# Hybrid decoder step: order of the query normalisation's first tiles, and where the first attention pair begins among dense pieces

## What is computed

```python
def trunk_layer(x, ...):
    xn = rmsnorm(x, norm_mix)
    lru_x, lru_g, q, k, v = jnp.split(xn @ w_in, SPLITS, axis=-1)
    xc = causal_conv(x_ext, w_conv, b_conv)
    hs, h_T = rg_lru(xc, pos, h0, ...)
    y_lru = (hs * jax.nn.gelu(lru_g)) @ w_branch_lru

    q = rmsnorm(q.reshape(B, T, N_ATT_HEADS, HEAD_DIM), q_gain)
    k = rmsnorm(k.reshape(B, T, N_ATT_HEADS, HEAD_DIM), k_gain)
    ...
        outs.append(dilated_attn_prompt(qg, kg, vg, tab, window, dil))
    ...
    o = combine_groups(outs)
    y_att = o @ w_branch_att
    g_lru, g_att = jnp.split(jax.nn.sigmoid(xn @ w_merge + b_merge), 2, axis=-1)
    x = x + (g_lru * y_lru + g_att * y_att) @ w_o
    gate, up = jnp.split(rmsnorm(x, norm_ffn) @ w_ffn_in, 2, axis=-1)
    return x + (jax.nn.silu(gate) * up) @ w_ffn_out, ...
```

## Time and profile before

| | |
|---|---|
| median of three runs | 2072.51 us (2072.47 to 2077.44) |
| the profiled execution | 2071.17 us |
| its span | 2069.4 us |
| PE busy | 2014.0 us (97%) |
| DVE, ACT, GpSimd busy | 905.9, 509.3, 552.1 us |
| PE clock granted, mean over the span | 0.993 of full |

### The profile page before, as it was taken

The page is one execution under the profiler, slowest core; times in us unless marked ns, Lnnn a source line. Parts: engine busy times, 40 slices in busy tenths (PEclk is TensorE's granted clock), DMA queues, the critical chain, the costliest instruction groups (busy, mean ns, idle before and its releaser), DMA issues.

```text
span 2069.4 us, 32282 instructions
## 1 busy us (share of the span) xinstructions
PE 2014.0 (97%) x12884; PEld 1952.3 (94%) x12884; DVE 905.9 (44%) x919; ACT 509.3 (25%) x726; POOL 552.1 (27%) x325
## 2 busy tenths in 40 slices
PE   7999998999989999999989899999999999999999
PEld 7999997999979999999978899999999999999999
DVE  6666677777762332222266553433311233212331
ACT  5366653333333433333311111201000000000000
POOL 2323332222211111111122143323323232323322
PEclk9999999999999999999999999999999999999999
DMA  5211111222223323334286361111111111111112
GB/s 200 97 44 43 43 46 61 93 90 81 101 97 135 116 97 136 114 111 149 87 307 236 125 239 51 44 48 51 41 51 41 51 42 49 51 41 51 41 59 84
DMA packets 71595, 188.45 MB, mean 91 GB/s; under 512 B 9313, under 2 KB 28796, under 8 KB 70780
## 3 DMA queue, kind: packets, MB, share of 16 engines
q1 hardware_dynamic: 41456, 136.97, 19.5%
q10 hardware_dynamic: 30092, 50.81, 6.7%
HBM read 145.09 MB, written 45.81 MB: 92 GB/s over the span
## 4 chain that ended last, share of the span: by engine, by line
PE 89%; DVE 6%; ACT 1%; issue 1%; DMA 1%; POOL 0%; ACTq 0%; SPq 0%; DVEq 0%; POOLq 0%
PE ups L472 64%; PE ups L600 13%; PE ups L625 3%; PE ups L650 3%; PE aux L637 2%; DVE x L1335 1%; PE aux L538 1%; PE aux L559 1%; PE ups L486 1%; PE aux L614 0%; DVE x L1489 0%; DVE x L1259 0%; DMA x<-o_s 0%; DVE x L1280 0%; ACT x L1076 0%
## 5 line engine op out<-in xcount | busy, mean ns | idle before, releaser
L472 PE MATMUL ups<-big,wsp 128*128 128x344 f32 x9216 | 1477.3, 321 | 9.1 <-POOL wsp L450 6.6
L472 PEld LDWEIGHTS ups<-big,wsp 128*128 128x128 f32 x9216 | 1459.4, 189 | 24.0 <-issue 16.9
L448 POOL CAST wsp<-wraw 128x1024 fp32r<-128x1024 f32 (+2 forms) x160 | 167.8, 1049 | 1485.0 <-issue 724.0
L450 POOL TENSOR_TENSOR wsp<-wraw,wsp 128x1024 fp32r<-128x1024 f32 (+2 forms) x160 | 384.0, 2400 | 12.8
L600 PE MATMUL ups<-big,wsp 128*128 128x344 f32 x1728 | 291.8, 324 | 0.0
L600 PEld LDWEIGHTS ups<-big,wsp 128*128 128x128 f32 x1728 | 272.7, 189 | 5.3 <-issue 5.2
L1335 DVE RECIPROCAL x<-x 128x1024 f32<-128x1024 f32 x24 | 157.3, 6553 | 74.4 <-ACT x L1006 74.4
L1372 DVE SCALAR_TENSOR_TENSOR x<-ups,ext 128x256 f32<-128x256 f32 (+1 forms) x96 | 48.0, 542 | 235.4 <-PE aux L637 147.4
L1181 ACT ACTIVATE ext<-ext 128x1032 f32<-128x1032 f32 x22 | 23.6, 1071 | 482.5 <-DVE ext L1589 482.4
L1591 DVE TENSOR_TENSOR ext<-ups,ext 128x1032 f32<-128x1032 f32 x22 | 27.1, 1233 | 215.4 <-PE ups L472 215.4
L1605 DVE TENSOR_TENSOR x<-ups,x 128x1032 f32 x24 | 29.6, 1233 | 203.6 <-PE ups L472 203.6
(11 more groups left out here) (190 smaller groups left out, 1147.9 us busy)
## 6 DMA issues: line engine op xcount, KB each, us to landing
wraw<-w_in SPq DMA_DIRECT2D x52, 512.0 KB, 3.4
wraw<-w_ffn_in SPq DMA_DIRECT2D x44, 512.0 KB, 3.2
out_qkv<-x ACTq DMA_DIRECT2D x28, 512.0 KB, 2.7
ext<-out_qkv SPq DMA_DIRECT2D x24, 512.0 KB, 4.3
x<-x_T SPq DMA_DIRECT2D x16, 516.0 KB, 8.2
x<-gate_s SPq DMA_DIRECT2D x16, 516.0 KB, 4.1
wraw<-w_merge SPq DMA_DIRECT2D x16, 512.0 KB, 4.9
wraw<-w_ffn_out SPq DMA_DIRECT2D x16, 512.0 KB, 3.5
```

The source lines that it names most:

```text
L448: nc.gpsimd.tensor_copy(hi, raw).then_inc(w_hi, 1)
L450: nc.gpsimd.tensor_tensor(lo, raw, hi.bitcast(F32), ALU.subtract).then_inc(w_split[slot], 1)
L472: ins = nc.tensor.matmul(ups[:, slot, c, 0:CH], wsp[:, slot, w, k, :], src[:, a, k, c * CH:(c + 1) * CH], start=(k == 0 and w + a == 0), s ...
```

## The change

Four edits, all of order:

- PE: in unit (1, 1), the sums of (0, 1) come before its first chunk and not after it; in the first attention pair 16 pieces (not 8) come ahead of the last sums, and `FIRST_PIECES` has 24 pieces (not 16) ahead of the value transposes, then 8, 4, 4, 3, 3 and 2 (before: 8, 8, 6, 4, 4 and 2).
- ACT: unit (0, 1) is copied out, squared and rounded ahead of the first root, with a wait for `z_done` that the old order did not need; the two output DMAs go behind that root.
- DVE: the first iteration of the loop is written out with both square differences one place earlier: those of (0, 1) ahead of the reciprocal of (0, 0), those of (1, 0) ahead of the reciprocal of (0, 1).

```diff
-        FIRST_PIECES = (16, 24, 32, 38, 42, 46, 48)
+        FIRST_PIECES = (24, 32, 36, 40, 43, 46, 48)
...
             unit("qk", 1, 0, big1, parts=(1, 2))
-            unit("qk", 1, 1, big1, parts=(0,))
             stats(1, 0)
-            unit("qk", 1, 1, big1, parts=(1,))
+            unit("qk", 1, 1, big1, parts=(0, 1))
             stats(0, 1)
...
-                    pieces(0, 8)
+                    pieces(0, 16 if first else 8)
                     if first:
                         stats(1, 11)
-                        pieces(8, marks[0])
+                        pieces(16, marks[0])
...
             evac(0, 0)
+            act.wait_ge(z_done, KT + 1)
+            evac(0, 1)
             act.wait_ge(lru_done, KT)
+            root(0, 0)
             act.dma_start(O["lru_out"], sout[:]).then_inc(out_done, 16)
             act.dma_start(O["state_out"], stc[:]).then_inc(out_done, 16)
-            root(0, 0)
-            evac(0, 1)
...
-            with dve.Fori(0, 11) as i:
-                step.loop(i, 2)
+            square_low(0, 1)
+            normed_qk(0, 0)
+            square_low(1, 0)
+            normed_qk(0, 1)
+            with dve.Fori(1, 11) as i:
+                step.loop(i, 2, 1)
                 normed_qk(i, 0)
                 square_low(i, 1)
                 normed_qk(i, 1)
                 square_low(i + 1, 0)
-            step.end(11)
+            step.end(10)
```

## The result

| | before | after |
|---|---|---|
| median of 13 runs | 2073.03 us (2070.33 to 2077.44) | 2077.46 us (2074.99 to 2083.23) |
| ratio | | 1.0023, 95% interval 1.0013 to 1.0032 |
| profiled execution, its span | 2071.17, 2069.4 us | 2075.36, 2073.6 us |

The change makes the kernel slower, by 4.4 us between the medians and by 4.8 by the ratio (2.7 to 6.6 by its interval). I had forecast 2072.3, practically no change, and a range up to 2076.8, which the time missed by 0.7 us. Two single executions in the experiments, 2198 us of the kernel before and 2464 us of part 2 filled, had a far lower granted clock (0.85 and 0.75) and are left out of the ratios.

A forecast was written before the change was run, and what follows sets the result against it. TensorE was taken to bound the kernel (89% of the chain), time counting only where it waits or runs at a lower clock. Terms -4.5 + 4.3 = -0.2 us from 2072.51 gave 2072.3 us, range 2067.8 to 2076.8.

The forecast's parts named there:

- Part 1: Start of the query-key stage: second sums without wait, 0.5 us before the third, 4.7 before the fourth; net gain 4.5 us.
- Part 2: First attention head pair: no wait for the last sums, 4.9 us for the scores, then a new wait; net loss 4.3 us.
- the gate of 4.32 on ACT's copy: First pair: pieces behind the first scores wait for ACT's copy L1046, made after the exponentials; forecast 4.2 us.
- The rival that the gate does not bind: First pair: copy L1046 isn't what pieces 24 to 32 wait for, so no cost there; 2068.0 us, chance 10%.
- the line for DVE: Query-key stage: DVE owes two reciprocals with L1337 (6.55 + 1.29 each) and one L1270, ending at 335.7; new wait 4.7 us.
- the one where I bounded the overlap with GpSimd by 0 and 0.5 and took 0: First pair: GpSimd's next weight split may lie beside DVE's last L1337; bounds 0 and 0.5 us, taken as 0.
- The gain of part 1 doesn't come: Rival, query-key stage: DVE makes the sums of (1,1) no earlier than before; +4.3, 2076.8 us, chance 12%.
- The clock stays low through the pair: Rival, first attention pair: after two long waits PE's clock stays low; +14, 2086 us, chance 5%.
- the 2.2 + 2.3 of the forecast: Prices of a clock fall at long PE waits: 2.2 us in the query-key stage, 2.3 us in the first attention pair.

The follow-up runs named there:

- part 2 filled: Only the attention change on the kernel before, with unread matmuls in PE's waits (16, 36, 34, 24): 1.0011, median 2075.02 us without the execution of 2464 us.
- the experiment without it: Changed kernel with no pieces behind the first scores, FIRST_PIECES = (24, 24, 33, 38, 44, 47, 48): 0.9992 of the kernel before, median 2071.93 us.
- the square difference in between: Changed kernel with DVE's square difference of (1,0) between reciprocal and product of (0,1), not ahead of the reciprocal: 1.0000 of the kernel before, median 2073.57 us.
- part 2 alone: The kernel before with only the attention change, 16 pieces ahead of the last sums and the new FIRST_PIECES: 1.0050, median 2083.7 us of 5 runs.
- the repaired kernel: Changed kernel with square difference between reciprocal and product, three GpSimd splits held back, no pieces behind first scores: 0.9965 of the kernel before, median 2066.11 us.
- one filled kernel: Changed kernel with matmuls that no one reads in PE's three long waits (36, 36, 24): 1.0002 of the kernel before, median 2072.93 us.

## Why the prediction was right or wrong

- **The order of the waits, right.** Part 1: no wait, 0.92 (forecast 0.5), then a new long one. Part 2: no wait for the last sums, the score wait, the gate of 4.32 on ACT's copy, then three waits at the transposes. The rival that the gate does not bind fell with the row itself, and the experiment without it gave 5.1 us of the pair back.
- **Part 1's size, wrong: 1.7 us of gain and not 4.5.** The step that failed is the line for DVE with L1337 at 1.29 us throughout. I noted GpSimd for part 2 alone and did not ask what it does when the unit (1,1) ends: its split is released by that unit's end, at 323.8, and DVE was by then so late that L1337 stood there, at 325.3. Before, L1337 of (0,1) was done, at 326.8, long before its split began at 335.2. L1337 lost 0.53 and 2.0 us. The first of these could be read ahead of the run: I had put L1337 of (0,0) at 312.7 to 314.1, and the trace before has this there:

```profile
311.05 2.40 POOL L450 TENSOR_TENSOR wsp<-wraw,wsp 128x1024 fp32r<-128x1024 f32 x1
```

  For the two together the fourth sums came 2.4 us later than forecast; with 0.5 for a longer fall of the clock (2.08 and 13.1 us behind the wait against 2.07 and 12.5), 4.5 becomes 1.6. With the splits held back the stage gained 4.4.
- **Part 2's size, wrong: 7.0 us of loss and not 4.3.** The step that failed is the one where I bounded the overlap with GpSimd by 0 and 0.5 and took 0. It was 1.21 us (L1337 2.50). The bound came from one row, 1.75 us beside 0.67 us of overlap, without asking how much overlap there could be. My own figures had some: L1337 due at 595.65 + 0.97 = 596.6, the split's end near 597. In that time (the attention's first piece laid on that of before, 1.97 us later) the split ended at 597.9 and L1337 began at 596.5. Second, the 24 matmuls behind the gate took 6.75 us for 5.54: +1.2. That there are two waits ahead of them and not one does not explain it, since three other kernels with the same two waits had 5.51, 5.53 and 5.70; here is that with the splits held back:

```profile
605.44 5.53 PE L612 MATMUL ups<-big,wsp 128*128 128x344 f32 x24 [4.33 <-ACT x L1059]
```

  In those three the clock fell a second time later in the pair, and the pair was no shorter for it (61.10 us with the square difference in between). So 5.54 was a fair price for these matmuls, and what was left out is a second fall behind the wait of 1.75 us or a longer first one. Another 0.4 lies between DVE's last instruction before the scores and the scores (0.45 us, 0.07 before). It belongs to part 1: all nine kernels with part 1 have 0.44 or 0.45 us there, and all four without it 0.07 or 0.08. Why, no run shows. 4.3 + 1.2 + 1.2 + 0.4 = 7.1.
- **The sum.** The signed forecast of -0.2 was the small difference of two terms of more than 4 us, and a missed 2.8 us in one and 2.7 in the other moved it wholly. Both errors have the same sign, and 3.6 of the 5.5 us have one root, L1337 beside a split; 1.7 are clock, 0.4 is open.
- **The rivals.** "The gain of part 1 doesn't come" named the mechanism, L1337 or its neighbours stretched beside the split, for the instructions L1286 to L1289, which took what they had taken before (of the two times I named, 2.65 us is beside a split; the 1.23 of L1289 begins after its end); it was worth 2.4 of the 4.3 us that I gave it. "The clock stays low through the pair" came in part: 0.59 granted for 7 us behind the gate, then 1.00. Its 14 us did not come.
- **The clock.** The fall was rightly put at the long waits, and filling them was worth 4.4 and 5.6 us in the two kernels, with intervals that hold the 2.2 + 2.3 of the forecast. It does not make the loss: that is there with the waits filled.

## What to carry to other kernels

When an edit moves a two-input VectorE instruction, look up what GpSimd does at its new time, by what releases each GpSimd instruction, and price the overlap by its length. Work that is to fill a gap can cost more than the gap when it waits itself: the pieces put behind the first scores waited for ACT's copy, which ACT makes only after the exponentials of those scores, and they held up the second scores and the transposes that stand behind them in PE's order. A forecast that is the difference of two large terms needs a range as wide as the terms' errors, not as their difference.

## What the runs showed of the hardware

**L1337 stands still while GpSimd's L450 runs, and ends 1.08 us behind it.** In the two traces 0.67 us of overlap cost 0.46, 0.74 cost 0.53, 1.38 cost 1.19, 1.42 cost 1.21 and 2.21 cost 2.0: each time the overlap less 0.2 us. In other words, whenever L450 was there first, L1337 ended 1.07 to 1.10 us behind the end of L450, wherever it had begun; that holds for all 25 overlaps in the thirteen traces between 280 and 640 us. With no overlap it took 1.28 or 1.29 us. So the price of an overlap is its length, and not a share of the instruction. L450 itself took 2.34 to 2.41 us in these, as it does alone. The reciprocal, one input, took 6.54 to 6.55 us beside the same split (305.82 in the trace after, with L450 from 310.75). The Trainium skill ("SBUF — State Buffer", "Who interferes with whom") says that a VectorE instruction with two SBUF inputs contends with a GpSimd instruction that reads SBUF, and one with a single input outside the two-port modes does not; the traces agree with both.

**Where the clock falls is not set by the wait's length alone.** Waits of 3.01 us and 2.69 us left it at 1.00 in the trace before, while in other executions it fell at or just behind the same waits (2.69 above, and 2.99 in the trace of part 2 alone, where the sums behind it took 2.07 us):

```profile
316.48 2.07 PE L559 MATMUL aux<-ext_r,bones_r 128*128 128x512 f32 x4 [2.99 <-DVE ext_r L1270]
```

One of 3.55 us left it up until just behind it in the repaired kernel, and one of 1.75 us was followed by a fall in one filled kernel and not in another. The Trainium skill ("TensorE: Matmul & The Clock Gate", Part 1) says that the activity window is free-running, which I had weighed as something that no trace here showed; these rows agree with it. It fits, too, that single executions of one kernel differ by 5 us and more: of the 13 executions of the changed kernel the longest, 2083.23 us, has the lowest mean granted clock, 0.986, and the shortest, 2074.99, has 0.992, the highest (correlation -0.90). That it is the window's phase that makes this difference, the runs don't prove.
